# A three-block network on one core: 1,152 bytes of gaps put between its buffers, and the weight places taken in another order

## The chip, the cores and the metric

The kernel runs on one core of a Trainium2 chip. The metric is the device time of one execution in microseconds (us); lower is better. A NeuronCore's on-chip memory (SBUF) has 128 partitions; every buffer here takes the same bytes in each partition, and "offset" below always means bytes within one partition, modulo 512.

## The reference, cut to what matters

Sequence of 512 tokens, width 1024, everything in float32. Two transformer layers and one mixed layer follow each other:

```python
# layer 0: latent attention (queries rank 384, keys/values rank 256, 8 heads), then MLP
# layer 1: sliding-window attention (16 query heads, 4 key heads), then MLP
x = _layernorm(alpha * x + y, ...)                     # y: attention output
x = _layernorm(alpha * x + relu(x @ w_up)**2 @ w_down, ...)   # 1024 -> 4096 -> 1024
# third layer: convolution branch and dilated attention, then a gated FFN (2816) and a gate
x = x + (silu(conv3(h @ w_gate)) * (h @ w_up)) @ w_down
x = x + sigmoid(rmsnorm(x) @ w_ple_gate) * (p @ w_ple_proj)
```

Nearly all of the work is the product of a weight matrix with activations of 512 tokens.

## The kernel before, in words

Activations lie transposed: features on partitions, tokens along the free axis, in tiles of 128 features by 512 tokens. A product in float32 precision is made of three TensorE matmuls in the float32r type: weights and activations are each split into a high and a low part, and `product` (L1721 to L1726) issues low x high (L1724), high x high (L1725) and high x low (L1726). The stationary operand of each is a block of 128x128 weights (512 bytes a partition), the moving operand is 512 tokens of one activation tile (2,048 bytes a partition), or 256 tokens in `half_gemm`. Each matmul loads its own stationary block (LDWEIGHTS), and that load runs beside the matmul before it.

The weights arrive as 148 slabs of 128x2048. SyncE issues one transfer for each into `stage[g % 2]`; ScalarE rounds it into `w_hi[place(g)]` (L429), VectorE puts the rest into `w_lo[place(g)]` (L929), and TensorE reads both (`gemm`, `half_gemm`, `values`). Places 0 and 1 alternate; place 2 (`w_hi2`, `w_lo2`, in the shared region) is used for eight slabs around the norms, the THIRDS. `values` turns a product round: there the activations are stationary and the weights move, 256 columns at a time.

The inputs of the products are `act_hi`/`act_lo` (normed activations), `hid_hi`/`hid_lo` (the MLP's inner layer), `h_hi`/`h_lo` (the FFN's), `o_hi`/`o_lo` (attention outputs), `c_hi`/`c_lo` (latents), and `p_hi`/`p_lo`. `act` lies in the fixed part of the memory that `keep` allocates one buffer after the other; all the others, and place 2, lie in one region behind it, laid out by `part`, in which several layouts share the same bytes over time. Buffers follow each other in the order of the calls. The sizes of stage, weight places, act and y are multiples of 512 bytes, so they all begin at one offset; `vec` (892 bytes) and the small buffers behind it set the offset of the shared region.

Of the kernel before, what the change touches and what calls it, by code (L numbers as in the profile page):

```python
# [9 lines left out]
F32 = mybir.dt.float32  # L10
F32R = mybir.dt.float32r

P = 128
T = 512
# [3 lines left out]
SLAB = 2048  # L18
# [137 lines left out]
def program(nc, slabs, x_t, ple_t, vecs, rel_bias, onehot, line_mask, rope, mats, causal, dilated, out):  # L156
    ctx = ExitStack()
    with ctx:
# [3 lines left out]
        def keep(name, shape, dt=F32):  # L162
            return ctx.enter_context(nc.sbuf_tensor(name, shape, dt))


        stage = [keep(f"stage{s}", [P, SLAB]) for s in range(2)]
        w_hi = [keep(f"w_hi{s}", [P, SLAB], F32R) for s in range(2)]
        w_lo = [keep(f"w_lo{s}", [P, SLAB], F32R) for s in range(2)]
        act_hi = keep("act_hi", [P, KT, T], F32R)
        act_lo = keep("act_lo", [P, KT, T], F32R)  # L170
        y = keep("y", [P, KT, T])
# [18 lines left out]
        sinkexp = keep("sinkexp", [P, 4 * 16])  # L190
        rden = keep("rden", [P, 4 * 16])
        negsink = keep("negsink", [P, 16])
        ps = ctx.enter_context(nc.psum_tensor("ps", [P, 8, BANK], F32))


# [2 lines left out]
        def part(floor, *specs):  # L198

            made = []  # L200
            with ExitStack() as shared:
                if floor:
                    floors[0] += 1
                    shared.enter_context(nc.sbuf_tensor(f"floor{floors[0]}", [P, floor], F32))
                for name, shape, dt in specs:
                    made.append(shared.enter_context(nc.sbuf_tensor(name, shape, dt)))
                    floor += int(np.prod(shape[1:]))
            return (*made, floor)

        (qr_hi, qr_lo, kn_hi, kn_lo, kr_hi, kr_lo, mv_hi, mv_lo, c_hi, c_lo, cossin, strip, top) = part(  # L210
            0, ("qr_hi", [P, 2, T], F32R), ("qr_lo", [P, 2, T], F32R), ("kn_hi", [P, 4, T], F32R),
            ("kn_lo", [P, 4, T], F32R), ("kr_hi", [P, T], F32R), ("kr_lo", [P, T], F32R),
            ("mv_hi", [P, 4, T], F32R), ("mv_lo", [P, 4, T], F32R), ("c_hi", [P, 5, T], F32R),
            ("c_lo", [P, 5, T], F32R), ("cossin", [P, 2, T], F32), ("strip", [P, T], F32))
        c_raw, rope_raw, rope_cos, rope_sin, _ = part(
            top, ("c_raw", [P, 5, T], F32), ("rope_raw", [P, T], F32), ("rope_cos", [P, T], F32),
            ("rope_sin", [P, T], F32))
        m_prob, m_pt_hi, m_pt_lo, _ = part(
            top, ("m_prob", [P, 2, CAUSAL.total], F32), ("m_pt_hi", [P, CAUSAL.total], F32R),
            ("m_pt_lo", [P, CAUSAL.total], F32R))  # L220
        hid_hi, hid_lo, relu, top = part(
            0, ("hid_hi", [P, KT, T], F32R), ("hid_lo", [P, KT, T], F32R), ("relu", [P, 2, 2, T], F32))
        strips, top_strips = part(top, ("strips", [P, SLAB], F32))
        w_hi2, w_lo2, _ = part(top_strips, ("w_hi2", [P, SLAB], F32R), ("w_lo2", [P, SLAB], F32R))
# [3 lines left out]
        swa_k_hi, swa_k_lo, _ = part(gap, ("swa_k_hi", [P, 2, T], F32R), ("swa_k_lo", [P, 2, T], F32R))  # L228
        dv_hi, dv_lo, top = part(gap, ("dv_hi", [P, 2, T], F32R), ("dv_lo", [P, 2, T], F32R))
# [5 lines left out]
        dq_hi, dq_lo, dk_hi, dk_lo, top = part(  # L235
            top_strips, ("dq_hi", [P, 2, T], F32R), ("dq_lo", [P, 2, T], F32R), ("dk_hi", [P, 2, T], F32R),
            ("dk_lo", [P, 2, T], F32R))
        u_pad, d_prob, d_pt_hi, d_pt_lo, rstd2, _ = part(
            top, ("u_pad", [P, 2, T + 2], F32), ("d_prob", [P, 2, CAUSAL.total], F32),
            ("d_pt_hi", [P, CAUSAL.total], F32R), ("d_pt_lo", [P, CAUSAL.total], F32R), ("rstd2", [P, T], F32))  # L240

        p_raw, p_hi, p_lo, mix_part, _ = part(
            top_strips, ("p_raw", [P, 2, T], F32), ("p_hi", [P, 2, T], F32R), ("p_lo", [P, 2, T], F32R),
            ("mix_part", [P, 2, T], F32))
        zc, conv, _ = part(0, ("zc", [P, 2, T], F32), ("conv", [P, 2, T], F32))
        yc, _ = part(KT * T, ("yc", [P, 4, T], F32))

        k_raw = d_prob[:, 0, 0:2 * T].rearrange("p (t c) -> p t c", t=2)
        h_hi, h_lo, top = part(0, ("h_hi", [P, FF_A, T], F32R), ("h_lo", [P, FF_A, T], F32R))
        gate, gconv, silu, ffh, top = part(  # L250
            top, ("gate", [P, 2, T + 2], F32), ("gconv", [P, 2, T], F32), ("silu", [P, 2, T], F32),
            ("ffh", [P, 2, T], F32))
        proj, _ = part(top, ("proj", [P, KT, T], F32))
        gate_in, _ = part(0, ("gate_in", [P, 2, 2, T], F32))
# [2285 lines left out]
```

How the kernel before makes its waits and increments, by code:

```python
        @block.sync  # L376
        def _(sp):
            for i, (a, b) in enumerate(PIECES):
                c = slice(2 * P * a, 2 * P * b)
                sp.dma_start(stage[0][:, c], slabs[0][:, c]).then_inc(first_landed[i], 16)
            sp.dma_start(stage[1][:, :], slabs[1]).then_inc(landed[1], 16)
            for dst, src in ((stat[0:32, 0:16], rel_bias), (sum2[0:32, 0:LINE], onehot),
                             (sum1[0:16, 0:LINE], line_mask), (vec[:, :], vecs), (mat[:, :, :], mats),
                             (cossin[:, :, :], rope), (strip[:, :], causal)):
                sp.dma_start(dst, src).then_inc(const_landed, 16)
            with sp.Fori(1, SLABS // 2) as n:
                for s in range(2):
                    sp.wait_ge(cast_lo, n * 2 + (s - 1))
                    sp.dma_start(stage[s][:, :], slabs[bass.ds(n * 2 + s, 1)].rearrange("a p w -> p (a w)"))\
                      .then_inc(landed[s], 16)
# [4 lines left out]
        @block.gpsimd  # L395
        def _(pool):
            nc.gpsimd.memset(tmp[:, 0, 0, 0:3 * P], 0.0).then_inc(warm_set, 1)
            nc.gpsimd.memset(eps[:, 0:1], LN_EPS).then_inc(eps_set, 1)
            nc.gpsimd.memset(eps[:, 1:2], RMS_EPS).then_inc(eps_set, 1)
            pool.wait_ge(slab_done, SWA_KV + 1)
            for v in (sv_hi, sv_lo):
                nc.gpsimd.memset(v[:, :, 64:128].bitcast(F32), 0.0).then_inc(v_zeroed, 1)
            pool.wait_ge(act_ready, LN_3 + 1)
```

## Time and profile before

| | |
|---|---|
| median of 3 runs | 1794.01 us (1793.74 to 1794.83) |
| the profiled execution's own time | 1793.78 us |
| its span, first to last instruction | 1792.0 us |
| TensorE busy | 1765.6 us (99%) |
| VectorE busy | 982.2 us (55%) |
| ScalarE busy | 670.9 us (37%) |
| mean granted TensorE clock | 0.998 of full |

How to read it: the span is the part of the time that the trace shows; 1.8 us of the profiled execution lie outside it. A matmul's duration in the trace includes its way through the array and overlaps the next one, so what a stream of matmuls costs is the distance from one start to the next, which the timeline gives: last start less first start, divided by the matmuls between them.

### The profile page before, as it was taken

What the parts mean: (1) busy time and instruction counts of PE and PEld (TensorE: products, weight loads), DVE (VectorE), ACT (ScalarE), POOL (GpSimd) and SP (SyncE); (2) the same over time, 40 slices, a digit from 0 to 9 for tenths busy, and PEclk for the clock granted to TensorE, in tenths of its full rate; (3) what the DMA queues carried; (4) which work ended last, traced back from release to release, by engine and by line L of the source; (5) the groups of instructions that cost most, each with busy time, mean ns of one, the idle gap of its engine ahead of it and who ended that gap; (6) DMA issues with size and microseconds to landing.
All of it is one profiled execution on the core that took longest, in us unless ns stands there. A gap on an engine that the chain in (4) does not pass through costs nothing.

```text
span 1792.0 us, 23527 instructions
## 1 busy us (share of the span) xinstructions
PE 1765.6 (99%) x9660; PEld 1505.9 (84%) x9660; DVE 982.2 (55%) x1437; ACT 670.9 (37%) x943; POOL 1.9 (0%) x11
## 2 busy tenths in 40 slices
PE   8899999999999999999999999999999999999999
PEld 6677998888889988998888889888888888888787
DVE  3666663333336666663333346757576666256654
ACT  3545442323234476442323134434355332122332
POOL 0000000000000000000000000000000000000000
PEclk9999999999999999999999999999999999999999
DMA  8211232222222211222222222221222222322341
GB/s 284 96 49 47 93 120 94 94 95 94 94 95 95 95 48 48 95 95 94 94 94 94 101 87 95 71 87 55 95 74 80 78 106 103 136 94 94 115 144 71
DMA packets 28885, 169.74 MB, mean 95 GB/s; under 512 B 2880, under 2 KB 7680, under 8 KB 9728
## 3 DMA queue, kind: packets, MB, share of 16 engines
q1 hardware_dynamic: 22592, 156.44, 24.4%
q10 hardware_dynamic: 6208, 12.08, 2.0%
q8 instruction: 64, 1.05, 0.2%
q14 instruction: 21, 0.17, 0.0%
HBM read 166.39 MB, written 5.27 MB: 96 GB/s over the span
## 4 chain that ended last, share of the span: by engine, by line
PE 90%; DVE 4%; ACT 3%; DMA 1%; issue 1%; SPq 0%; ACTq 0%; DVEq 0%
PE ps L1724 29%; PE ps L1726 28%; PE ps L1725 28%; PE ps L1857 2%; DVE w_lo L929 2%; ACT w_hi L429 1%; DMA stage<-slabs 1%; PE ps L1836 1%; PE ps L2070 0%; ACT y L586 0%; PE ps L1797 0%; PE ps L2202 0%; ACT act_hi L591 0%; PE ps L1977 0%; PE ps L2192 0%
## 5 line engine op out<-in xcount | busy, mean ns | idle before, releaser
L1724 PE MATMUL ps<-act_hi,w_lo 128*128 128x512 f32 (+1 forms) x1512 | 545.6, 361 | 7.8 <-DVE w_lo L929 2.5
L1726 PE MATMUL ps<-act_lo,w_hi 128*128 128x512 f32 (+1 forms) x1512 | 539.2, 357 | 0.0
L1725 PE MATMUL ps<-act_hi,w_hi 128*128 128x512 f32 (+1 forms) x1512 | 538.9, 356 | 0.0
L429 ACT ACTIVATE w_hi<-stage 128x2048 fp32r<-128x2048 f32 (+4 forms) x147 | 268.2, 1824 | 387.0 <-PE ps L1726 385.9
L929 DVE TENSOR_TENSOR w_lo<-stage,w_hi 128x2048 fp32r<-128x2048 f32 (+6 forms) x152 | 323.3, 2128 | 86.1 <-ACT w_hi L429 79.3
L1724 PEld LDWEIGHTS ps<-act_hi,w_lo 128*128 128x128 f32 x1512 | 285.3, 189 | 54.0 <-issue 8.7
L1726 PEld LDWEIGHTS ps<-act_lo,w_hi 128*128 128x128 f32 x1512 | 285.1, 189 | 41.7
L1725 PEld LDWEIGHTS ps<-act_hi,w_hi 128*128 128x128 f32 x1512 | 285.1, 189 | 39.8
L1724 PE MATMUL ps<-hid_hi,w_lo 128*128 128x512 f32 (+1 forms) x608 | 218.4, 359 | 2.1 <-DVE w_lo L929 2.1
L1726 PE MATMUL ps<-hid_lo,w_hi 128*128 128x512 f32 (+1 forms) x608 | 216.9, 357 | 0.0
L1725 PE MATMUL ps<-hid_hi,w_hi 128*128 128x512 f32 (+1 forms) x608 | 215.3, 354 | 0.0
L1724 PEld LDWEIGHTS ps<-hid_hi,w_lo 128*128 128x128 f32 x608 | 114.4, 188 | 18.2 <-issue 2.4
L1726 PEld LDWEIGHTS ps<-hid_lo,w_hi 128*128 128x128 f32 x608 | 114.2, 188 | 18.3
L1725 PEld LDWEIGHTS ps<-hid_hi,w_hi 128*128 128x128 f32 x608 | 114.3, 188 | 17.6
L1156 DVE TENSOR_TENSOR relu<-relu 128x1024 f32<-128x1024 f32 x32 | 39.2, 1224 | 142.0 <-ACT relu L622 136.3
L1036 DVE TENSOR_TENSOR y<-y,ps 128x1024 f32<-128x1024 f32 (+1 forms) x30 | 30.2, 1006 | 111.4 <-PE ps L1726 111.4
L622 ACT ACTIVATE relu<-ps 128x1024 f32<-128x1024 f32 x26 | 26.7, 1027 | 167.0 <-PE ps L1726 167.0
L1724 PE MATMUL ps<-h_hi,w_lo 128*128 128x512 f32 x176 | 69.2, 393 | 2.5 <-DVE w_lo L929 2.0
L1726 PE MATMUL ps<-h_lo,w_hi 128*128 128x512 f32 x176 | 69.1, 393 | 0.0
L1725 PE MATMUL ps<-h_hi,w_hi 128*128 128x512 f32 x176 | 68.6, 390 | 0.0
L1724 PE MATMUL ps<-o_hi,w_lo 128*128 128x256 f32 (+1 forms) x176 | 60.4, 343 | 0.6 <-DVE y L1035 0.6
L929 DVE TENSOR_TENSOR hid_lo<-relu,hid_hi 128x1024 fp32r<-128x1024 f32 x32 | 39.2, 1225 | 36.0 <-ACT hid_hi L625 36.0
(296 smaller groups left out, 2185.3 us busy)
## 6 DMA issues: line engine op xcount, KB each, us to landing
stage<-slabs SPq DMA_DIRECT2D x147, 1024.0 KB, 4.8
bias_rows<-bias_line ACTq DMA_DIRECT2D x1, 3072.0 KB, 16.7
strips<-dilated ACTq DMA_DIRECT2D x2, 1024.0 KB, 4.9
y<-x_t ACTq DMA_DIRECT2D x3, 512.0 KB, 8.8
out<-y ACTq DMA_DIRECT2D x3, 512.0 KB, 2.6
strips<-bias_rows ACTq DMA_DIRECT2D x1, 1024.0 KB, 5.4
strips<-bias_rows ACTq DMA_DIRECT2D x2, 512.0 KB, 3.9
stage<-slabs SPq DMA_DIRECT2D x3, 256.0 KB, 8.4
```

The costliest lines, as they stand in the source:

```text
L429: nc.scalar.activation(w_hi[p][:, 0:w], stage[s][:, 0:w], ACT.Copy).then_inc(cast_hi, 1)
L622: nc.scalar.activation(relu[:, j % 2, :, :], ps[:, b:b + 2, :], ACT.Relu)\
L929: return nc.vector.tensor_tensor(dst, src, f32(hi), ALU.subtract)
L1036: return nc.vector.tensor_tensor(part, part, source, ALU.add)
L1156: nc.vector.tensor_tensor(relu[:, j % 2, :, :], relu[:, j % 2, :, :], relu[:, j % 2, :, :], ALU.mult).then_inc(sqr_done, 1)
L1724: mm(out, l_lo, r_hi, start=start, stop=False, skip_group_check=shared)
L1725: mm(out, l_hi, r_hi, start=False, stop=False, skip_group_check=shared)
L1726: return mm(out, l_hi, r_lo, start=False, stop=stop, skip_group_check=shared)
L1836: last = [nc.tensor.matmul(o, part[l], part[r], start=x == 0, stop=x == 2) for o, part in zip(outs, parts)]
L1857: last = nc.tensor.transpose(ps[:, a.trans_bank + n, c:c + P], prob[:, u % 2, k:k + P], ident)
```

## The change

Nothing in the order of the work, in the instructions, their shapes or their waits is touched. Only addresses move. The allocation order becomes `w_hi0, w_lo0, gap of 448, w_hi1, w_lo1, gap of 128`; a gap of 320 bytes stands before the shared region; and a gap of 256 stands between `mv_lo` and `c_hi`.

```diff
-        w_hi = [keep(f"w_hi{s}", [P, SLAB], F32R) for s in range(2)]
-        w_lo = [keep(f"w_lo{s}", [P, SLAB], F32R) for s in range(2)]
+        w_hi, w_lo = [], []
+        for s in range(2):
+            w_hi.append(keep(f"w_hi{s}", [P, SLAB], F32R))
+            w_lo.append(keep(f"w_lo{s}", [P, SLAB], F32R))
+            keep(f"apart{s}", [P, (448, 128)[s] // 4])
...
         negsink = keep("negsink", [P, 16])
+        keep("apart2", [P, 320 // 4])
...
-            ("mv_hi", [P, 4, T], F32R), ("mv_lo", [P, 4, T], F32R), ("c_hi", [P, 5, T], F32R),
-            ("c_lo", [P, 5, T], F32R), ("cossin", [P, 2, T], F32), ("strip", [P, T], F32))
+            ("mv_hi", [P, 4, T], F32R), ("mv_lo", [P, 4, T], F32R), ("apart3", [P, 256 // 4], F32),
+            ("c_hi", [P, 5, T], F32R), ("c_lo", [P, 5, T], F32R), ("cossin", [P, 2, T], F32), ("strip", [P, T], F32))
```

The offsets modulo 512 at which the buffers begin, before as allocated, after by adding the gaps that come to stand ahead of each:

| buffer | before | gaps ahead | after |
|---|---|---|---|
| stage 0, 1 | 128 | 0 | 128 |
| place 0 (w_hi0, w_lo0) | 128 | 0 | 128 |
| place 1 (w_hi1, w_lo1) | 128 | 448 | 64 |
| act_hi, act_lo, y | 128 | 576 | 192 |
| hid, h, o, p, mv, kn, place 2 | 448 | 896 | 320 |
| c_hi, c_lo | 448 | 1152 | 64 |

Every block of 128 weights and every tile of 256 or 512 tokens begins a multiple of 512 bytes behind its buffer's start, so one number describes a pair: how far the moving operand begins behind the stationary one, modulo 512.

| moving with stationary | before | after |
|---|---|---|
| act with place 0 / 1 / 2 | 0 / 0 / 192 | 64 / 128 / 384 |
| hid, h, o, p with place 0 / 1 / 2 | 320 / 320 / 0 | 192 / 256 / 0 |
| c with place 0 / 1 | 320 / 320 | 448 / 0 |
| place 0 with c | 192 | 64 |
| place 0 / 1 with act (`values`) | 0 / 0 | 448 / 384 |

## Rows read from the trace of the kernel before

**Rows 1.** The page: busy time, clock by fortieths, the chain, a group of loads.

```profile
PE 1765.6 (99%) x9660; PEld 1505.9 (84%) x9660; DVE 982.2 (55%) x1437; ACT 670.9 (37%) x943; POOL 1.9 (0%) x11
...
PEclk9999999999999999999999999999999999999999
...
PE 90%; DVE 4%; ACT 3%; DMA 1%; issue 1%; SPq 0%; ACTq 0%; DVEq 0%
...
L1724 PEld LDWEIGHTS ps<-act_hi,w_lo 128*128 128x128 f32 x1512 | 285.3, 189 | 54.0 <-issue 8.7
```

**Rows 2.** TensorE's groups by shape; L1725 and L1726 each have as many.

```profile
L1724 PE MATMUL ps<-act_hi,w_lo 128*128 128x512 f32 x1048 | 412.3, 393 | 5.8 <-DVE act_lo L929 2.4 <-DVE mark L1401 1.8 <-DVE w_lo L929 1.6
...
L1724 PE MATMUL ps<-hid_hi,w_lo 128*128 128x512 f32 x416 | 163.9, 394 | 0.0
L1724 PE MATMUL ps<-act_hi,w_lo 128*128 128x256 f32 x464 | 133.2, 287 | 2.0 <-DVE act_lo L933 1.0 <-DVE w_lo L929 0.9
...
L1724 PE MATMUL ps<-h_hi,w_lo 128*128 128x512 f32 x176 | 69.2, 393 | 2.5 <-DVE w_lo L929 2.0 <-DVE h_lo L929 0.5
...
L1724 PE MATMUL ps<-hid_hi,w_lo 128*128 128x256 f32 x192 | 54.5, 284 | 2.1 <-DVE w_lo L929 2.1
...
L1724 PE MATMUL ps<-o_hi,w_lo 128*128 128x512 f32 x80 | 33.1, 414 | 0.0
...
L1724 PE MATMUL ps<-w_hi,act_lo 128*128 128x256 f32 x96 | 27.8, 290 | 0.6 <-DVE y L1036 0.6
L1724 PE MATMUL ps<-o_hi,w_lo 128*128 128x256 f32 x96 | 27.3, 284 | 0.6 <-DVE y L1035 0.6
...
L1724 PE MATMUL ps<-c_hi,w_lo 128*128 128x512 f32 x52 | 22.9, 440 | 2.3 <-DVE c_lo L929 2.3
```

**Rows 3.** Timeline, act with place 1, 512 wide: first and last of 177.

```profile
1400.03 0.39 PE L1726 MATMUL ps<-act_lo,w_hi 128*128 128x512 f32 x1
...
1439.92 0.39 PE L1725 MATMUL ps<-act_hi,w_hi 128*128 128x512 f32 x1
```

**Rows 4.** Timeline, h with place 1, 512 wide: first and last of 176.

```profile
1519.86 0.39 PE L1725 MATMUL ps<-h_hi,w_hi 128*128 128x512 f32 x1
...
1559.91 0.39 PE L1726 MATMUL ps<-h_lo,w_hi 128*128 128x512 f32 x1
```

**Rows 5.** Timeline, place 0 moving, c stationary: first and last of 23.

```profile
135.27 0.39 PE L1724 MATMUL ps<-w_hi,c_lo 128*128 128x512 f32 x1
...
140.40 0.39 PE L1725 MATMUL ps<-w_hi,c_hi 128*128 128x512 f32 x1
```

**Rows 6.** Timeline, act with place 0, 256 wide: first and last of 69.

```profile
1115.13 0.28 PE L1725 MATMUL ps<-act_hi,w_hi 128*128 128x256 f32 x1
...
1123.30 0.28 PE L1724 MATMUL ps<-act_hi,w_lo 128*128 128x256 f32 x1
```

**Rows 7.** Timeline, act with place 2, 256 wide: first and last of 47.

```profile
782.04 0.28 PE L1724 MATMUL ps<-act_hi,w_lo 128*128 128x256 f32 x1
...
787.46 0.28 PE L1725 MATMUL ps<-act_hi,w_hi 128*128 128x256 f32 x1
```

**Rows 8.** Timeline, o with place 1, 256 wide: first and last of 75.

```profile
733.13 0.28 PE L1725 MATMUL ps<-o_hi,w_hi 128*128 128x256 f32 x1
...
741.52 0.28 PE L1724 MATMUL ps<-o_hi,w_lo 128*128 128x256 f32 x1
```

**Rows 9.** One tile's instructions (durations ns min/median/max): both halves of a slab's split.

```profile
L929 DVE TENSOR_TENSOR w_lo<-stage,w_hi x152: 425/2291/2294, 5.6 to 1771.3; 128x2048 fp32r<-128x2048 f32 x127, 128x1536 fp32r<-128x1536 f32 x6, 128x1280 fp32r<-128x1280 f32 x6, 128x1152 fp32r<-128x1152 f32 x4
...
L429 ACT ACTIVATE w_hi<-stage x147: 1058/1911/1942, 15.7 to 1769.4; 128x2048 fp32r<-128x2048 f32 x127, 128x1536 fp32r<-128x1536 f32 x6, 128x1280 fp32r<-128x1280 f32 x6, 128x1152 fp32r<-128x1152 f32 x4
```

More of the change, by code:

```diff
@@ L208, in part @@
             return (*made, floor)
-        (qr_hi, qr_lo, kn_hi, kn_lo, kr_hi, kr_lo, mv_hi, mv_lo, c_hi, c_lo, cossin, strip, top) = part(
+        (qr_hi, qr_lo, kn_hi, kn_lo, kr_hi, kr_lo, mv_hi, mv_lo, _, c_hi, c_lo, cossin, strip, top) = part(
             0, ("qr_hi", [P, 2, T], F32R), ("qr_lo", [P, 2, T], F32R), ("kn_hi", [P, 4, T], F32R),
             ("kn_lo", [P, 4, T], F32R), ("kr_hi", [P, T], F32R), ("kr_lo", [P, T], F32R),
-            ("mv_hi", [P, 4, T], F32R), ("mv_lo", [P, 4, T], F32R), ("c_hi", [P, 5, T], F32R),
-            ("c_lo", [P, 5, T], F32R), ("cossin", [P, 2, T], F32), ("strip", [P, T], F32))
+            ("mv_hi", [P, 4, T], F32R), ("mv_lo", [P, 4, T], F32R), ("apart3", [P, 256 // 4], F32),
+            ("c_hi", [P, 5, T], F32R), ("c_lo", [P, 5, T], F32R), ("cossin", [P, 2, T], F32), ("strip", [P, T], F32))
         c_raw, rope_raw, rope_cos, rope_sin, _ = part(
```

## The prediction

> **What bounds the kernel now.** I read the page first. TensorE is busy for 1765.6 of 1792.0 us at the upper level of its clock (2.4 GHz) in all forty slices, and the chain that ended last runs through it for 90% [rows 1]. So the time is the sum of what TensorE's matmuls cost, and the question is whether that cost depends on an address. The groups by shape say what there is [rows 2]: three lines of `product` with 1048 matmuls each on act, 512 tokens wide, 416 on hid, 176 on h, 80 on o, 52 on c; 256 wide 464 on act, 192 on hid, 96 on o, and 96 with the weights moving.
>
> A matmul's own duration (393 ns) overlaps its neighbour, so I took undisturbed stretches of the timeline and divided. At 2.4 GHz 512 columns take 213.3 ns and 256 take 106.7 ns; what lies above is the excess.
>
> - act with place 1, 0 bytes apart: (1439.92 - 1400.03) / 176 = 226.6 ns, excess 13.3 [rows 3]
> - h with place 1, 320 apart: (1559.91 - 1519.86) / 175 = 228.9 ns, excess 15.5 [rows 4]
> - place 0 with c, 192 apart: (140.40 - 135.27) / 22 = 233.2 ns, excess 19.9 [rows 5]
> - 256 wide, act with place 0, 0 apart: 8.17 us / 68 = 120.1 ns, excess 13.5 [rows 6]
> - 256 wide, act with place 2, 192 apart: 5.42 us / 46 = 117.8 ns, excess 11.1 [rows 7]
> - 256 wide, o with place 1, 320 apart: 8.39 us / 74 = 113.4 ns, excess 6.7 [rows 8]
>
> The same instructions of the same shape differ by 6.6 ns, and they sort by distance. The excess of four of the six is close to 6.7, 13.3 or 20 ns, one, two or three times 16 columns (6.67 ns, or 64 bytes of the moving tile); the two others lie between. I read this as a meeting of two reads: the moving operand and the stationary block of the next matmul, which is being loaded meanwhile (189 ns [rows 1]). Where they meet depends on the distance, and one or more such steps are paid. That is an inference from six stretches, not something that the trace shows by itself.
>
> The Trainium skill says otherwise: "TensorE: Matmul & The Clock Gate", section "Step-by-step: what each phase is for", has TensorE reading SBUF through two independent ports, so that loading the next weights takes no bandwidth from the running matmul. By that rule the whole change is worth nothing. This trace does not agree: equal shapes run at 113.4 and 120.1 ns [rows 6, 8].
>
> **The change part by part.** It adds and removes no instruction, wait or transfer, so every price is a number of matmuls times a difference of their distance from start to start. The numbers by place come from `place(g)`.
>
> *act, 512 wide:* 3 x 1048 = 3144 matmuls, 1632 on place 0 (0 apart becomes 64) and 1512 on place 1 (0 becomes 128). Neither distance occurs before. Bounds: one step over the stream, 220.0 ns, as the 256-wide stretch reaches [rows 8], gives -6.6 x 3144 = -20.8 us; the dearest row, 233.2 ns [rows 5], gives +20.8 us. The nearest row says little: 0 apart is two steps in both widths, and the only state with one step is found at a distance other than 0. I take it that one of the two places comes down by a step and the other stays: -6.6 x 1572 = -10.4 us. This is the choice on which the forecast stands.
>
> *act, 256 wide on places 0 and 1, and weights moving over act:* 3 x 464 - 480 = 912, and 3 x 96 = 288, together 1200 at 120.1 ns, all leaving 0 apart. Nearest row 117.8 ns [rows 7]: -2.3 x 1200 = -2.8 us. Bounds: 0 and, with 113.4 ns, -8.0 us.
>
> *act, 256 wide on place 2:* 480, 192 apart becomes 384. I take 0; bounds -4.4 x 480 = -2.1 and +2.3 x 480 = +1.1 us.
>
> *hid, h and o, 512 wide:* 3 x (416 + 176 + 80) = 2016, now all at 228.9 ns [rows 4]. On place 0 there are 936, which come to 192 apart, the distance of the row with 233.2 ns [rows 5]: +4.3 x 936 = +4.0 us; bounds -8.3 (220.0 ns) and +4.0. On place 1 there are 1080, which come to 256 apart, a distance without a row: I take 0; bounds -9.6 and +4.6 us.
>
> *hid and o, 256 wide:* 576 on places 0 and 1 stay among distances that run at 113.4 or 117.8 ns: 0; bounds -2.5 and +2.5. The 288 on place 2 keep their 0.
>
> *c:* 156 moving and 48 stationary, 512 wide; 102 come to 0 apart (-2.3 x 102 = -0.2 us) and the 48 leave 192 (up to -13.2 x 48 = -0.6). I take -0.4 us; bounds -2.0 and +0.7.
>
> *Other engines:* stage and place 1 come 64 bytes apart, stage and place 2 go from 320 to 192. ScalarE's and VectorE's halves of a split take 1911 and 2291 ns in the median and at most 1942 and 2294 [rows 9], with places 0 and 1 at 0 and place 2 at 320 from stage among them. So their prices don't feel the distance: 0. Their cover is the slab before, of 48 matmuls at 227 ns, 10.9 us; were it gone, each slab would pay what the split takes, but 4.2 us against 10.9 leaves it in place. The transfers into stage keep their addresses; x and the output move with y by 64 bytes, and lie within the DMA's 1% of the chain.
>
> Sum: -10.4 - 2.8 + 0 + 4.0 + 0 + 0 - 0.4 = -9.6 us. The profiled execution took 1793.78 us, span 1792.0 and 1.8 outside it, and lies 0.2 us below the median: 1793.8 - 9.6 = 1784.2, and 1784.4 on the scale of the medians.
>
> **Rivals.**
>
> *The new distances are dear (slower).* For it: of the three 512-wide rows the one at 0 apart is the cheapest, and both distances other than 0 cost more [rows 3, 4, 5]. If act goes to 228.9 ns at both places: +2.3 x 3144 = +7.2, and with -2.8 + 4.0 - 0.4 it is +8.0: 1802. If it goes to 233.2 ns: 20.8 + 0.8 = +21.6: 1815.6. The terms besides act sum to +0.8, so it is decided where act's mean at 512 leaves 226.6: by 0.25 ns down it is even, above that slower. Against it: the 256-wide rows are in the other order, 0 apart the dearest [rows 6, 7, 8], and the steps are the same there.
>
> *More than one place gains (much faster).* Both places at 220.0 ns: -20.8 - 2.8 + 4.0 - 0.4 = -20.0, 1774; if hid, h and o on place 1 gain a step too (-9.6), 1764. Against it: no 512-wide row shows one step.
>
> *Nothing changes.* The excess would belong to the kind of operand or to how a stretch began, not to the distance. For it: hid and act differ in more than their distance. Against it: act itself runs at 120.1 ns with place 0 and at 117.8 ns with place 2 [rows 6, 7]. The time would be 1794.
>
> **How the numbers follow.** One step at one place, the forecast: 0.32, with a range of its own of 1777 to 1791. Much faster, below 1777: 0.20. Nothing, within 0.2% (3.6 us, about what the measurement can tell from no change): 0.12. Slower: 0.36, of it 0.24 about 1802 and 0.12 about 1816. Faster is 0.32 + 0.20 = 0.52. I leave out the far end of much faster, below 1767 (0.09), and of slower, above 1811 (0.10), and give 1767 to 1811; all bounds at once would reach from 1741 to 1827, but they would all have to fall on one side.
>
> **What would show it.** In the trace after: stretches of act, 512 wide, near 220 ns on one place and 226.6 on the other; act and moving weights, 256 wide, near 117.8; hid, h and o on place 0 at 233.2, on place 1 at 228.9; hid with place 2 unchanged at 120; the splits unchanged at 1911 and 2291 ns. The forecast is wrong if act at 64 and 128 apart lies at 229 ns or more, or if the distance between starts isn't a matter of distance in bytes.

## The result, and the profile after

The changed kernel is slower: 1810.97 us in the median of 4 runs (1809.61 to 1811.5) against 1793.88 us before, ratio 1.0092 with a 95% interval of 1.0077 to 1.0107. The forecast of 1784.4 had the wrong sign; the time is near the dear end of the first rival, 1815.6, and at the upper edge of the range (1811).

The page of the changed kernel, its busy times, its clock and its chain, to be held against [rows 1]:

```profile
PE 1783.5 (99%) x9660; PEld 1510.2 (83%) x9660; DVE 982.0 (54%) x1437; ACT 670.9 (37%) x943; POOL 1.9 (0%) x11
...
PE 91%; DVE 4%; ACT 3%; DMA 1%; issue 1%; SPq 0%; ACTq 0%; DVEq 0%
```

TensorE is busy for 17.9 us more with as many matmuls, and the span is longer by 17.1 us (1809.1 against 1792.0). VectorE and ScalarE are busy as long as before. One tile's view of the two halves of a slab's split, VectorE's and ScalarE's, against [rows 9]:

```profile
L934 DVE TENSOR_TENSOR w_lo<-stage,w_hi x152: 424/2291/2294, 5.6 to 1788.1; 128x2048 fp32r<-128x2048 f32 x127, 128x1536 fp32r<-128x1536 f32 x6, 128x1280 fp32r<-128x1280 f32 x6, 128x1152 fp32r<-128x1152 f32 x4
L434 ACT ACTIVATE w_hi<-stage x147: 1055/1913/1943, 15.9 to 1786.2; 128x2048 fp32r<-128x2048 f32 x127, 128x1536 fp32r<-128x1536 f32 x6, 128x1280 fp32r<-128x1280 f32 x6, 128x1152 fp32r<-128x1152 f32 x4
```

So the added time lies in TensorE's stream. The timeline of the changed kernel (called "after" from here on) shows where. Each pair of lines is the first and the last matmul of a stretch, 512 wide, of 46, 46, 34 and 34 matmuls: act with place 1, 128 bytes apart; act with place 0, 64 apart; h with place 0, 192 apart; h with place 1, 256 apart.

```profile
1052.46 0.40 PE L1730 MATMUL ps<-act_hi,w_hi 128*128 128x512 f32 x1
...
1062.97 0.39 PE L1730 MATMUL ps<-act_hi,w_hi 128*128 128x512 f32 x1
...
1063.65 0.39 PE L1730 MATMUL ps<-act_hi,w_hi 128*128 128x512 f32 x1
...
1073.95 0.39 PE L1730 MATMUL ps<-act_hi,w_hi 128*128 128x512 f32 x1
...
1572.34 0.39 PE L1730 MATMUL ps<-h_hi,w_hi 128*128 128x512 f32 x1
...
1580.04 0.40 PE L1730 MATMUL ps<-h_hi,w_hi 128*128 128x512 f32 x1
...
1580.74 0.39 PE L1730 MATMUL ps<-h_hi,w_hi 128*128 128x512 f32 x1
...
1588.24 0.39 PE L1730 MATMUL ps<-h_hi,w_hi 128*128 128x512 f32 x1
```

By the same division as in the prediction: 10.51 us / 45 = 233.6 ns, 10.30 / 45 = 228.9, 7.70 / 33 = 233.3 and 7.50 / 33 = 227.3. Before, act was at 226.6 [rows 3] and h at 228.9 [rows 4]. (The stretches of [rows 3, 4, 6, 8] are headed with one place but run on over both in turn; the two places lay at the same distance then, so the prices stand.) The 256-wide stretches: act with place 2, 384 apart, 46 matmuls; place 0 moving over act, 448 apart, 44; o with place 1, 256 apart, 45.

```profile
786.42 0.28 PE L1730 MATMUL ps<-act_hi,w_hi 128*128 128x256 f32 x1
...
791.76 0.28 PE L1730 MATMUL ps<-act_hi,w_hi 128*128 128x256 f32 x1
...
1302.74 0.28 PE L1731 MATMUL ps<-w_lo,act_hi 128*128 128x256 f32 x1
...
1307.62 0.28 PE L1729 MATMUL ps<-w_hi,act_lo 128*128 128x256 f32 x1
...
756.02 0.28 PE L1731 MATMUL ps<-o_lo,w_hi 128*128 128x256 f32 x1
...
761.30 0.28 PE L1730 MATMUL ps<-o_hi,w_hi 128*128 128x256 f32 x1
```

5.34 / 45 = 118.7 ns where it was 117.8 [rows 7], 4.88 / 43 = 113.5, and 5.28 / 44 = 120.0 where it was 113.4 [rows 8].

A smaller part lies in the clock. The trace of after has three stretches at the lower level (1.2 GHz) where that of before has none; two more, at 50 and 57 us, both traces have. Windows of after (us of the stretch, TensorE busy and its matmuls, granted clock, DMA share, GB/s):

```profile
1196.90:1200.30 3.40, 3.40 (x18) 0.50 0.29 67
...
1295.90:1299.30 3.40, 3.40 (x17) 0.50 0.00 0
...
1708.90:1712.30 3.40, 3.40 (x9) 0.50 0.69 239
1712.30:1716.00 3.70, 3.70 (x18) 1.00 0.58 166
```

In the last one 9 matmuls are at work in 3.4 us, in the 3.7 us behind it 18, so a stretch can cost half its length, 1.7 us. Both traces hold the same 9660 matmuls in the same order, so that each start can be held against its partner's: by that the three stretches cost 0.9, 1.5 and 1.6 us, 4.0 together. Ahead of the falls at 1196.9 and 1295.9 lie sixteen matmuls of two columns in 1.95 and 2.00 us, ahead of that at 1708.9 a wait of 1.34 us for `w_lo`; the same instructions lie there in the trace of before, where the clock stayed up.

### The profile page after: what moved, and what is told of

Read it like the earlier page. It is cut to its first block, busy times and chain, and to the rows that moved or that the text cites. A ratio compares the mean times of both kernels' runs of the same rounds, so it can differ in the third digit from the quotient of the medians.

```text
span 1809.1 us, 23527 instructions
## 1 busy us (share of the span) xinstructions
PE 1783.5 (99%) x9660; PEld 1510.2 (83%) x9660; DVE 982.0 (54%) x1437; ACT 670.9 (37%) x943; POOL 1.9 (0%) x11
## 4 chain that ended last, share of the span: by engine, by line
PE 91%; DVE 4%; ACT 3%; DMA 1%; issue 1%; SPq 0%; ACTq 0%; DVEq 0%
PE ps L1729 29%; PE ps L1730 28%; PE ps L1731 28%; PE ps L1862 2%; DVE w_lo L934 1%; ACT w_hi L434 1%; DMA stage<-slabs 1%; PE ps L1841 1%; PE ps L2075 0%; ACT y L591 0%; PE ps L1802 0%; PE ps L2207 0%; PE ps L2197 0%; ACT act_hi L596 0%; PE ps L1982 0%
## 6 DMA issues: line engine op xcount, KB each, us to landing
bias_rows<-bias_line ACTq DMA_DIRECT2D x1, 3072.0 KB, 16.2
```

## Experiments

Two theories stood against each other after the result. DISTANCE: the price of a matmul depends on how far its moving operand begins behind the stationary block that is loaded meanwhile, modulo some period. PLACES or SURROUNDINGS: what costs is something else that the layout moved, such as the weight places against stage, or the other engines' reads and writes.

**e1_distances: the price by itself.** All else is taken out: one core runs matmuls alone, and the distance is a slice's start.

```diff
+            def stretch(d, width):
+                for k in range(KT):
+                    for m in range(2):
+                        c = (2 * k + m) * P
+                        a = k * T + d // 4
+                        o = ps[:, m, 0:width]
+                        mm(o, w_lo[:, c:c + P], m_hi[:, a:a + width], start=k == 0, stop=False)
+                        mm(o, w_hi[:, c:c + P], m_hi[:, a:a + width], start=False, stop=False)
+                        last = mm(o, w_hi[:, c:c + P], m_lo[:, a:a + width], start=False, stop=k == KT - 1)
```

> A kernel of matmuls alone, nothing of the reference computed: in the pattern of product (low x high, high x high, high x low, a block of 128 weights loaded for each) it runs stretches of 48 matmuls, the moving tile beginning 0 to 496 bytes (in steps of 16) behind the weights modulo 512, 512 wide, then the multiples of 64 in falling order, then both orders 256 wide. No other engine works meanwhile. Theory DISTANCE (the price of a matmul depends on how far its moving tile begins behind the next block of weights, modulo 512): 512 wide 226.7 ns at 0, 229 at 64, 233.3 at 128, 233.4 at 192, 227.2 at 256, 229 at 320, about 233 at 448, as the two kernels' stretches have it; 256 wide 120 at 0 and 117.8 or 113.4 at 192, 320; the falling order gives the same. Rival SURROUNDINGS (ScalarE's and VectorE's reads and writes at other offsets, or the buffers' places in memory, make the price): the same gap at every distance, near one value between 216 and 227 ns.

Its timeline, first and last of 46 matmuls each, 512 wide at 0, 64, 128, 192 and 256 bytes:

```profile
459.22 0.40 PE L69 MATMUL ps<-m_hi,w_hi 128*128 128x512 f32 x1
...
469.43 0.39 PE L69 MATMUL ps<-m_hi,w_hi 128*128 128x512 f32 x1
...
69.68 0.39 PE L69 MATMUL ps<-m_hi,w_hi 128*128 128x512 f32 x1
...
79.98 0.39 PE L69 MATMUL ps<-m_hi,w_hi 128*128 128x512 f32 x1
...
437.06 0.39 PE L69 MATMUL ps<-m_hi,w_hi 128*128 128x512 f32 x1
...
447.51 0.40 PE L69 MATMUL ps<-m_hi,w_hi 128*128 128x512 f32 x1
...
158.86 0.39 PE L69 MATMUL ps<-m_hi,w_hi 128*128 128x512 f32 x1
...
169.35 0.40 PE L69 MATMUL ps<-m_hi,w_hi 128*128 128x512 f32 x1
...
203.40 0.40 PE L69 MATMUL ps<-m_hi,w_hi 128*128 128x512 f32 x1
...
213.63 0.39 PE L69 MATMUL ps<-m_hi,w_hi 128*128 128x512 f32 x1
```

Divided by 45: 226.9, 228.9, 232.2, 233.1 and 227.3 ns. The whole table, from the starts of 40 matmuls in the middle of each stretch (one execution; 512 wide 64 to 448 from the rising pass and 0 from the falling one, 256 wide the rising pass):

| bytes apart | 0 | 64 | 128 | 192 | 256 | 320 | 384 | 448 |
|---|---|---|---|---|---|---|---|---|
| 512 wide, ns | 226.7 | 228.8 | 232.5 | 233.3 | 226.9 | 228.8 | 232.5 | 233.3 |
| 256 wide, ns | 120.0 | 117.8 | 118.7 | 113.3 | 119.9 | 117.8 | 118.7 | 113.3 |

512 wide these are the prices of the two kernels to about 1 ns, with no other engine at work: DISTANCE holds and SURROUNDINGS falls. e1 moves only the moving operand, so alone it can't tell a distance from that operand's own address; after can: there act begins at one address and costs 228.9 ns with place 0 and 233.6 with place 1. The table repeats after 256 bytes. Of the 32 distances in steps of 16 bytes, none is under 226.6 ns at 512 wide; 0, 240, 256 and 496 reach it, and the dearest are 208 and 464 with 234.7.

256 wide the table isn't that of the kernels: before has 117.8 ns at 192 apart [rows 7] and 113.4 at 320 [rows 8], where e1 has 113.3 and 117.8, the other way round. What lies behind that came out with e5 and e6.

**e2_act_128, e8_act_64, e7_act_256: act alone, by three amounts.** The order of the places, their offset to stage and the shared region stay.

```diff
+        keep("apart1", [P, 128 // 4])   # 64 in e8, 256 in e7
         act_hi = keep("act_hi", [P, KT, T], F32R)
...
         negsink = keep("negsink", [P, 16])
+        keep("apart2", [P, 384 // 4])   # 448 in e8, 256 in e7
```

> The kernel before with act (and y, tmp, vec and what lies behind them) 128 bytes on, and the shared region back at 320 from the weights: only act's distance to places 0 and 1 changes, 0 to 128, and that to place 2, 192 to 320. Theory DISTANCE: 3144 matmuls of act 512 wide at 233.3 instead of 226.7 ns = +20.8 us, 1200 that are 256 wide at 118.6 instead of 120 (those of the weights moving, at 384, too) = -1.7 us, so about +19 us, 1813. Rival PLACES (the order of the weight places and their offset to stage, or the shared region, cost the 17 us): 1794, within 2 us. Rival CLOCK (what the change costs is the two more stretches of half clock in the trace, not the stream): no more than +5 us.

Measured: 1810.67 us, ratio 1.009 (1.0074 to 1.0107).

> The kernel before with act and what lies behind it 64 bytes on, the shared region back at its offset: act is 64 instead of 0 from places 0 and 1, 256 instead of 192 from place 2. Theory DISTANCE, prices from the stretches of matmuls alone: 3144 x (228.8 - 226.7) = +6.6 us, 1200 that are 256 wide at 117.8 instead of 120 (the 288 with weights moving at 448: 117.8 or 113.3) = -2.6 to -3.9 us, 480 on place 2 at 119.9 instead of 117.8 = +1.0: +3.7 to +5.0 us, 1798 to 1799.5, about a quarter of what 128 bytes cost. Rival APART BY ANY AMOUNT (leaving the common offset costs the same whatever the distance): 1810, as with 128. Rival NONE: 1794.

Measured: 1798.92 us, ratio 1.0023 (1.0013 to 1.0034).

> The kernel before with act and what lies behind it 256 bytes on, the shared region back at its offset: act is 256 instead of 0 from places 0 and 1 and 448 instead of 192 from place 2. Theory DISTANCE with the period of 256: act's stretches on places 0 and 1 stay at 226.7 to 227 and 120 ns, on place 2 they go from 117.8 to 113.3 ns (480 x 4.5 = -2.1 us): about 1792. Rival APART (any beginning apart of act and weights costs as 128 did): 1805 to 1811.

Measured: 1794.01 us, ratio 1.0001 (0.9992 to 1.001). The timelines of act with place 1 in e2 and with place 0 in e8 and e7, 512 wide, 46 matmuls each:

```profile
1052.45 0.40 PE L1727 MATMUL ps<-act_hi,w_hi 128*128 128x512 f32 x1
...
1062.92 0.39 PE L1727 MATMUL ps<-act_hi,w_hi 128*128 128x512 f32 x1
```

```profile
1058.38 0.39 PE L1727 MATMUL ps<-act_hi,w_hi 128*128 128x512 f32 x1
...
1068.68 0.39 PE L1727 MATMUL ps<-act_hi,w_hi 128*128 128x512 f32 x1
```

```profile
1056.29 0.39 PE L1727 MATMUL ps<-act_hi,w_hi 128*128 128x512 f32 x1
...
1066.48 0.39 PE L1727 MATMUL ps<-act_hi,w_hi 128*128 128x512 f32 x1
```

That is 232.7, 228.9 and 226.4 ns: the table's values to 0.5 ns. 64 bytes cost 0.23%, 128 cost 0.9%, 256 nothing. This alone rules out that beginning apart is what costs, and that the moved places do. The sum for e2 (+19) was 3 us too high, that for e8 (+3.7 to +5.0) held, and in e7 the 2 us expected from act on place 2 did not come: its eight stretches stayed at 117.8 ns. (e2's expectation counts two stretches of half clock in the trace of after; there are three.)

**e3_region_192: the shared region alone.**

```diff
         negsink = keep("negsink", [P, 16])
+        keep("apart2", [P, 384 // 4])
```

> The kernel before with the shared region alone moved by 384 bytes: hid, h, o, p, c come to 192 instead of 320 from places 0 and 1; act stays at 0 from them, and comes to 320 from place 2. Theory DISTANCE: 2016 matmuls of hid, h and o and 156 of c, 48 of p, 512 wide, at 233.4 instead of 228.9 ns = +10.0 us, 256 wide about 0: 1804. Rival PLACES: 1794, within 2 us. Rival CLOCK: no more than +5 us and no difference in the stretches.

Measured: 1802.94 us, ratio 1.0052 (1.0036 to 1.0069). h with place 0, 34 matmuls:

```profile
1566.28 0.39 PE L1726 MATMUL ps<-h_hi,w_hi 128*128 128x512 f32 x1
...
1573.98 0.39 PE L1726 MATMUL ps<-h_hi,w_hi 128*128 128x512 f32 x1
```

233.3 ns, as the distance of 192 has it. The granted clock of its profiled execution is 0.998, that of before, so here the stream alone costs the 8 us, and CLOCK falls as the main cause. The time is about 1 us under the 1804 expected; one part is that act on place 2, at 320 apart, came down to 113.3 ns in five of its eight stretches, where 256 wide about 0 was expected.

**e4_all_aligned: the opposite of the change.**

```diff
         negsink = keep("negsink", [P, 16])
+        keep("apart2", [P, 192 // 4])
```

> The kernel before with the shared region moved by 192 bytes, so that every moving operand begins 0 bytes from every weight place: the opposite of beginning apart. Theory DISTANCE: 2016 + 156 + 48 matmuls at 226.7 instead of 228.9 ns = -4.9 us; 576 that are 256 wide at 120 instead of 117.8 or 113.4 = +1.3 to +2.5 us, 480 on place 2 at 120 instead of 117.8 = +1.1 us: -1.3 to -2.5 us, about 1792. Rival APART (it is good to begin apart, and only the particular distances of the change were bad): slower than before, by 5 us or more.

Measured: 1790.63 us, ratio 0.9985 (0.9975 to 0.9994), the first layout that is faster than before, by a little more than the sum had it. Of its ten runs the six under 1791 us have a granted clock of 0.998, the four above 1792 one of 0.995 to 0.997. h with place 0 goes from 228.9 to 7.48 us / 33 = 226.7 ns:

```profile
1556.79 0.39 PE L1726 MATMUL ps<-h_hi,w_hi 128*128 128x512 f32 x1
...
1564.27 0.39 PE L1726 MATMUL ps<-h_hi,w_hi 128*128 128x512 f32 x1
```

**e5_place2_64 and e6_fine_256: the layout meant to be best, and why it gives less.** Place 2 is read 256 wide only, so its distance can be chosen for that width.

```diff
         negsink = keep("negsink", [P, 16])
+        keep("apart2", [P, 192 // 4])
...
-        hid_hi, hid_lo, relu, top = part(
+        hid_hi, hid_lo, relu, _, top = part(
...
+            ("apart4", [P, 64 // 4], F32))
...
-        proj, _ = part(top, ("proj", [P, KT, T], F32))
+        _, proj, _ = part(top, ("apart5", [P, 64 // 4], F32), ("proj", [P, KT, T], F32))
```

> The kernel with everything aligned, and place 2 (with what shares its bytes, and the last layer's inputs p) 64 bytes on: act and hid, which meet place 2 only 256 wide, then begin 448 bytes behind its weights. Theory DISTANCE, prices from the stretches of matmuls alone (256 wide 113.3 at 448, 120 at 0): 768 matmuls on place 2 come from 120 to 113.3 ns = -5.1 us against the aligned kernel, 48 of p at 229 instead of 226.7 = +0.1: about 1785.5, ratio 0.9955 to before. Rival LIMIT (256-wide stretches are short and never settle, or the engines beside them wash it out): no more than 1 us below the aligned kernel's 1790.6.

Measured: 1789.74 us, ratio 0.9977 (0.9968 to 0.9986). That is the lowest median here, about 1 us under e4 where 5 were expected; the two intervals overlap, so the times don't show e5 to be faster than e4. Its act on place 2, 448 apart, 46 matmuls:

```profile
781.26 0.28 PE L1727 MATMUL ps<-act_hi,w_hi 128*128 128x256 f32 x1
...
786.56 0.28 PE L1727 MATMUL ps<-act_hi,w_hi 128*128 128x256 f32 x1
```

117.8 ns, not the 113.3 of e1 at this distance. With 2.2 ns less than the 120.0 of e4 instead of 6.7, 768 matmuls give 1.7 us instead of 5.1. e6 is e1 with other stretches (256 wide in steps of 16 bytes, then both widths in steps of 4).

> Matmuls alone again (nothing of the reference computed), stretches of 48: 256 wide at 0 to 496 bytes in steps of 16, then both widths from 448 to 524 in steps of 4. Theory DISTANCE with a period of 256 bytes: 256 wide the same table in both halves, 120 at 0 and 256, 113.3 at 192 and 448; 512 wide 233.3 at 448 falling to 226.7 at 496. Rival PERIOD 512: the halves differ. Open, and wanted for a layout: whether some distance is at its floor in both widths (512 wide 226.7 at 496 already; if 256 wide is 113.3 there too, 1776 matmuls on places 0 and 1 could gain 6.7 ns each, 11.8 us).

It passed the distance of 448 at 256 wide twice, after another 256-wide stretch and after a 512-wide one (46 matmuls each):

```profile
183.56 0.28 PE L68 MATMUL ps<-m_hi,w_hi 128*128 128x256 f32 x1
...
188.67 0.28 PE L68 MATMUL ps<-m_hi,w_hi 128*128 128x256 f32 x1
...
429.44 0.28 PE L68 MATMUL ps<-m_hi,w_hi 128*128 128x256 f32 x1
...
434.75 0.28 PE L68 MATMUL ps<-m_hi,w_hi 128*128 128x256 f32 x1
```

5.11 / 45 = 113.6 and 5.31 / 45 = 118.0 ns at one distance: 256 wide the stream has two states here, settles into one within its first few matmuls (in the first pass the distances from start to start are 119, 122 and 116 ns, then 113 or 114) and keeps it to the end of the stretch. The kernels show the same, and at other distances. act with place 2, 320 apart, behind act with place 1, first in e3 and then in e2 (46 matmuls each):

```profile
216.54 0.28 PE L1726 MATMUL ps<-act_hi,w_hi 128*128 128x256 f32 x1
...
221.64 0.28 PE L1726 MATMUL ps<-act_hi,w_hi 128*128 128x256 f32 x1
```

```profile
217.53 0.28 PE L1727 MATMUL ps<-act_hi,w_hi 128*128 128x256 f32 x1
...
222.83 0.28 PE L1727 MATMUL ps<-act_hi,w_hi 128*128 128x256 f32 x1
```

5.10 / 45 = 113.3 and 5.30 / 45 = 117.8 ns. In the traces of all runs both prices occur at 64, 192, 320 and 448 apart, and at no other multiple of 64: in e8 act at 64 apart runs at 113.3 on place 0 and mostly at 117.8 on place 1. So the two orders of before and e1 are two draws of one pair of states. What picks the state isn't shown; in e6 the two passes differ in the stretch ahead of them, but so few passes prove no rule.

At 496 bytes 512 wide is at 226.7 ns, but 256 wide at 117.1, not at 113.3; the 11.8 us hoped for are not to be had there. But the last part of e6 has better than beginning together (0 apart: 226.7 and 120.0 ns). At 492 bytes, 512 wide and 256 wide, 46 matmuls each:

```profile
329.91 0.39 PE L68 MATMUL ps<-m_hi,w_hi 128*128 128x512 f32 x1
...
340.11 0.39 PE L68 MATMUL ps<-m_hi,w_hi 128*128 128x512 f32 x1
...
492.22 0.28 PE L68 MATMUL ps<-m_hi,w_hi 128*128 128x256 f32 x1
...
497.42 0.28 PE L68 MATMUL ps<-m_hi,w_hi 128*128 128x256 f32 x1
```

10.20 / 45 = 226.7 and 5.20 / 45 = 115.6 ns. An estimate: the 912 + 576 matmuls, 256 wide, of act, hid and o on places 0 and 1 would gain 4.4 ns each, 6.5 us against e4. The 288 with the weights moving would then lie 20 bytes apart, which no run has. No kernel was run with such a layout. The 256-wide table repeats after 256 bytes too.

## Why the prediction was wrong, point by point

**What bounds the kernel** was right: TensorE's stream set the time, and all 17 us came there.

**That the price follows the distance** was right 512 wide. 256 wide it was right in part: the two rows that made the 256-wide order, 117.8 ns [rows 7] and 113.4 ns [rows 8], are the two states of a stream, not the prices of 192 and 320 apart. The Trainium skill's page "TensorE: Matmul & The Clock Gate", section "Step-by-step: what each phase is for", says that loading the next weights takes no read bandwidth from the running matmul. The runs bear out the prediction's doubt that the change is then worth nothing: with TensorE alone at work, matmuls of one shape take 226.7 to 234.7 ns each by the distance. That it is the load that holds up the running matmul, the meeting of two reads of the prediction, was argued and not shown: no run leaves the loads out.

**The step that failed** is the first term, act 512 wide: "I take it that one of the two places comes down by a step and the other stays: -6.6 x 1572 = -10.4 us". Neither came down. Place 0 (64 apart) went to 228.9 ns, +2.3 x 1632 = +3.8 us, and place 1 (128 apart) to 233.6, and to 233.2 in the mean of its 22 undisturbed stretches of 48, +6.6 x 1512 = +10.0 us: together +13.8 where -10.4 stood. The floor of one step, 220.0 ns, was carried over from a 256-wide row [rows 8] to the 512-wide shape. No distance tried reaches it: of the 32 in steps of 16 bytes the least is 226.6. Before the change act already lay on that floor [rows 3]; the three 512-wide rows said so, as the rival noted, and were outweighed by rows of the other width.

**hid, h and o on place 0:** +4.0 forecast; 233.3 instead of 228.9 ns, +4.4 x 936 = +4.1 us. Right. On place 1 0 was taken; it was a gain, 227.3 instead of 228.9, -1.6 x 1080 = -1.7 us, inside the bounds.

**256 wide:** act on places 0 and 1, and the weights over act, -2.8 forecast. By the stretches (117.8 at 64, 118.7 at 128 and 384, 113.5 at 448) it is -2.2 x 480 - 1.3 x 432 - 6.5 x 192 - 1.3 x 96 = -3.0 us. The terms taken as 0 were mis-sized: act on place 2 +0.9 x 480 = +0.4; o on place 1 came from 113.4 to 120.0, +6.6 x 96 = +0.6, and hid there from 117.8 to 120, +2.2 x 192 = +0.4.

**Other engines** at 0: right (2291 ns in both).

These products of price and number sum to 13.8 + 4.1 - 1.7 - 3.0 + 1.4 = +14.6 us, and the three stretches at half clock, at 1.7 us each, would add 5.1: 19.7 against the 17.1 measured. Held against each other start by start, the two traces show where the products are too high. The half clock cost 4.0. act 512 wide on place 0 costs 3.7 us more, as in the product, but on place 1 only 7.6: its 22 undisturbed stretches (1056 matmuls) carry 6.5 of it, the other 456 matmuls, most of them in stretches cut up by waits and other matmuls, 1.1, that is 2.4 ns each and not 6.6. So act's two places cost 11.4 us and not 13.8, and e2's sum was too high in the same term: 15.3 there instead of 20.8, in part because act ran at 232.4 ns there and not at 233.3. That makes 16.2 of the 17.1 us; the rest is spread over small groups. A product of price and number needs the number of matmuls in undisturbed stretches.

Whether the layout brings the stretches at half clock stays open. The four runs of after have a mean granted clock of 0.994 to 0.996, the kernel before 0.996 to 0.998 in all runs made beside the experiments; but e2 reaches 0.997 in two of its four runs, and kernels with the same layout vary as much.

The first rival, slower, was right in its mechanism, that the new distances are dear, and in its turning point: act's mean at 512 went above 226.6, and that decided. Its two cases priced both places alike; the change has one of each.

## What to carry to other kernels

A stream of float32r matmuls with a new block of weights each is priced by where the moving operand begins against the stationary one, modulo 256 bytes. 512 wide, beginning both at the same offset is at the floor of 226.7 ns, as are 240 and 496 apart; the other distances in steps of 16 bytes cost 0.9 to 3.5% more. Beginning buffers "apart" is no virtue: the faster layouts are the one with all operands aligned (e4, 0.9985) and that one with the place that is read 256 wide shifted (e5, 0.9977), and the runs don't tell these two apart. When a floor is read from rows, take it from the same shape; and price a layout with a small kernel of stretches, which gives the whole table in one run. Before trusting such a price, see whether the same distance has it in several stretches of the real kernel.

## What the runs showed of the hardware that was not expected

- The 512-wide price falls into a few values: 226.7, 228.8 and a group from 231 to 234.7 ns in steps of 16 bytes; in steps of 4 bytes it jumps between neighbours, from 226.7 at 496 to 240.0 at 500 and 230.0 at 504.
- 256 wide the order is another: 0 and 256 apart are among the dearest (120.0 ns), 112, 192 and their like plus 256 the cheapest (113.3).
- At one distance, 256 wide, two steady states were seen, 113.3 and 117.8 ns. e1 and e6 have both at 448 apart; the kernels have both at 64, 192 and 320 too.
